# Expert rows as quarter rows, turned by a VectorE block transpose instead of TensorE transposes

## What is computed

```
s = sigmoid(h @ router_w)                    # 384 tokens x 64 experts, 8 chosen per token
for each expert e, on the rows xb of h that chose it:
    y = (silu(xb @ wg[e]) * (xb @ wu[e])) @ wd[e]      # 1024 -> 256 -> 1024
out = swiglu(h, sh_w_gate, sh_w_up, sh_w_down) + sum over a token's experts of weight * y
```

## Time and profile before

| | us |
|---|---|
| runs: median (lowest, highest of 3) | 1751.35 (1750.44, 1751.37) |
| profiled execution: span, first to last instruction | 1745.4 |
| PE busy | 1661.9 (95%) |
| DVE busy | 642.6 (37%) |
| ACT busy | 387.3 (22%) |
| POOL busy | 222.8 (13%) |
| data moved | 530.52 MB |

### The profile page before, as it was taken

The page is one execution under the profiler, slowest core; times in us unless marked ns, Lnnn a source line. Parts: engine busy times, 40 slices in busy tenths (PEclk is TensorE's granted clock), DMA queues, the critical chain, the costliest instruction groups (busy, mean ns, idle before and its releaser), DMA issues.

```text
span 1745.4 us, 22336 instructions
## 1 busy us (share of the span) xinstructions
PE 1661.9 (95%) x8468; PEld 821.2 (47%) x8468; DVE 642.6 (37%) x1697; ACT 387.3 (22%) x842; POOL 222.8 (13%) x217
## 2 busy tenths in 40 slices
PE   4999889989999999999979998998999999999997
PEld 2765344644444444444447553555434444444443
DVE  2479372522222222222256765442322222222222
ACT  2410343221111111111152104431111111111111
POOL 0200010011111111111113000101111111111110
PEclk7999999999999999999989999999999999999999
DMA  9312753399999999999932229017899999999994
GB/s 403 133 54 102 279 210 145 126 403 374 417 403 413 417 388 419 420 420 419 381 128 97 103 97 375 23 60 310 338 418 416 396 420 396 412 419 420 419 420 166
DMA packets 77291, 530.52 MB, mean 304 GB/s; under 512 B 10880, under 2 KB 14080, under 8 KB 21632
## 3 DMA queue, kind: packets, MB, share of 16 engines
q1 hardware_dynamic: 67392, 503.90, 70.7%
q0 software_dynamic: 9792, 25.18, 3.7%
HBM read 533.76 MB, written 5.77 MB: 309 GB/s over the span
## 4 chain that ended last, share of the span: by engine, by line
PE 89%; DVE 4%; DMA 4%; ACT 2%; issue 1%; SPq 0%; POOL 0%; DVEq 0%; ACTq 0%
PE PSB L932 30%; PE PSB L941 15%; PE PSB L924 7%; PE PSB L986 6%; PE PSB L987 5%; PE PSB L974 4%; PE PSB L860 4%; DMA RING<-in_wmod 2%; PE PSB L896 1%; PE PSB L959 1%; PE PSB L919 1%; PE PSB L680 1%; PE PSB L906 1%; PE PSB L897 1%; DMA RING<-in_exp_w_up 1%; PE PSB L948 1%
## 5 line engine op out<-in xcount | busy, mean ns | idle before, releaser
L932 PE MATMUL PSB<-WB,EX 128*32 128x512 f32 (+2 forms) x1408 | 431.9, 598 | 0.6 <-DMA RING<-in_exp_w_up 0.6
L932 PE MATMUL PSB<-RING,EX 128*32 128x512 f32 (+2 forms) x1344 | 417.2, 598 | 1.7 <-DVE EX L1790 1.7
L941 PE MATMUL PSB<-RING,AT 128*32 128x512 f32 (+2 forms) x720 | 227.9, 599 | 4.8 <-ACT GROW L1299 3.7
L1808 DVE TENSOR_TENSOR YL<-PSB,YH 128x512 fp32r<-128x512 f32 x136 | 94.1, 692 | 353.8 <-ACT YH L1380 353.8
L941 PE MATMUL PSB<-WB,AT 128*32 128x512 f32 (+2 forms) x704 | 210.8, 596 | 0.0
L564 POOL TENSOR_SCALAR SCAT<-CST,LSTT 128x384 fp32r<-128x384 f32 x68 | 85.1, 1251 | 833.0 <-PE PSB L987 832.8
L932 PEld LDWEIGHTS PSB<-WB,EX 128*32 128x32 f32 (+2 forms) x1408 | 113.1, 126 | 136.3 <-issue 136.3
L986 PE MATMUL PSB<-YH,SCAT 128*128 128x512 f32 x408 | 171.6, 421 | 2.8 <-DVE YL L1808 2.8
L1790 DVE COPY EX<-PSB 128x512 f32<-128x512 f32 x68 | 47.1, 692 | 317.4 <-PE PSB L974 317.4
L932 PEld LDWEIGHTS PSB<-RING,EX 128*32 128x32 f32 (+2 forms) x1344 | 105.8, 124 | 122.5 <-issue 122.5
L987 PE MATMUL PSB<-YL,SCAT 128*128 128x512 f32 x408 | 161.0, 395 | 0.0
(11 more groups left out here) (286 smaller groups left out, 1856.6 us busy)
## 6 DMA issues: line engine op xcount, KB each, us to landing
RING<-in_exp_w_gate SPq DMA_DIRECT2D x64, 1024.0 KB, 12.4
RING<-in_exp_w_up SPq DMA_DIRECT2D x64, 1024.0 KB, 14.7
RING<-in_exp_w_down SPq DMA_DIRECT2D x64, 1024.0 KB, 13.1
WB<-in_exp_w_gate SPq DMA_DIRECT2D x64, 1024.0 KB, 11.7
WB<-in_exp_w_up SPq DMA_DIRECT2D x64, 1024.0 KB, 14.4
WB<-in_exp_w_down SPq DMA_DIRECT2D x64, 1024.0 KB, 13.3
RING<-in_wmod SPq DMA_DIRECT2D x16, 2048.0 KB, 10.6
KSYS<-in_wmod SPq DMA_DIRECT2D x8, 2048.0 KB, 10.4
```

What stands on the lines that cost most here:

```text
L932: mm = nc.tensor.matmul(PS[6][s0:s0 + w, :].rearrange("p (w f) -> p w f", w=2), e[:, k, s0:s0 + w], rawgu[n % NBUF][:, k], start=(k == 0), ...
L941: mm = nc.tensor.matmul(dst[s0:s0 + w, :], AT[:, j, s0:s0 + w], rawdn[n % NBUF][:, hf, j], start=(j == 0), stop=(j == 1))
L1808: v.tensor_tensor(YLb[s % 2][:, hf * 512:(hf + 1) * 512], PS[6 + hf][:, :], YHb[s % 2][:, hf * 512:(hf + 1) * 512].bitcast(F32), ALU.subtr ...
```

## The change

A row of h is now gathered as four quarter rows of 1 KB. HTOK is written in a permuted order, so that quarter r of a row holds, for each of the eight k-blocks, 32 of its features. The gather uses four indirect DMAs: DMA g fills columns 256g to 256g + 255 of XG, and on partition 32r + j it brings quarter r of the token of slot 32g + j. A transpose of 32x32 blocks on DVE then gives EX2 directly: on partition 32r + i stands feature i of quarter r, and along the free axis the slots 32g + j. IDX becomes four columns, filled by sixteen small DVE operations on 32 partitions each (4 x token + r, from PSUM partitions 32g on to SBUF partitions 32r on). The eight transposes on PE, their copies on ACT and DVE and their semaphores go; PE waits for `d_ex` of the DVE transpose instead. The wait for the second YL half, which stood before the first transposes, stands after gate/up. The same is done in the `more` loop.

```diff
-LSTN, SORTN = 4, 10
+LSTN, SORTN = 19, 10
...
+        h_quarters = h_rows.rearrange("t (r n) -> (t r) n", r=4)
...
-            IDX = sb("IDX", [P, NU], mybir.dt.int32, c=me)
+            IDX = sb("IDX", [P, NU, 4], mybir.dt.int32, c=me)
...
                 pool.wait_ge(d_lst, LSTN * (NU * l + s + 1))
                 if s >= 2:
-                    pool.wait_ge(pe_rows, 2 * (NU * l + s - 1))
-                pool.indirect_dma_start(XG[:, s % 2, :], None, h_rows,
-                                        bass.IndirectOffsetOnAxis(ap=IDX[:, s:s + 1], axis=0),
-                                        bounds_check=TOK - 1, oob_is_err=False).then_inc(rows_in[s % 2], 16)
+                    pool.wait_ge(d_ex, NU * l + s - 1)
+                for g in range(4):
+                    pool.indirect_dma_start(XG[:, s % 2, g * 256:(g + 1) * 256], None, h_quarters,
+                                            bass.IndirectOffsetOnAxis(ap=IDX[:, s, g:g + 1], axis=0),
+                                            bounds_check=4 * TOK - 1, oob_is_err=False).then_inc(rows_in[s % 2], 16)
...
+            def slots(b):
+
+                return lambda k, s0, w: EX2[:, b, k, s0:s0 + w]
...
-            def rows(l, s, h):
-
-                if h == 0:
-                    pe.wait_ge(rows_in[s % 2], 16 * (len(range(s % 2, NU, 2)) * l + s // 2 + 1))
-                else:
-                    pe.wait_ge(e_low, NU * l + s + 1)
-                for c in range(4):
-                    k = 4 * h + c
-                    mm = nc.tensor.transpose(PS[7][:, c * P:(c + 1) * P], XG[:, s % 2, k * P:(k + 1) * P], ident)
-                mm.then_inc(pe_rows, 1)
...
-                pe.wait_ge(e_low, NU * l + s + 1)
-                pe.wait_ge(e_high, NU * l + s + 1)
+                pe.wait_ge(d_ex, NU * l + s + 1)
                 if s > 0:
                     pe.wait_ge(d_yl, 2 * (NU * l + s) - 1)
                 for k in range(KD):
-                    mm = gate_up(job, EX2[:, s % 2], k)
-                    if k == 2 and s + 1 < NU:
-                        if s > 0:
-                            pe.wait_ge(d_yl, 2 * (NU * l + s))
-                        rows(l, s + 1, 0)
-                    if k == 5 and s + 1 < NU:
-                        rows(l, s + 1, 1)
+                    mm = gate_up(job, slots(s % 2), k)
                 mm.then_inc(pe_gu, 1)
-                if s + 1 < NU:
-                    pe.wait_ge(e_high, NU * l + s + 2)
+                if s > 0:
+                    pe.wait_ge(d_yl, 2 * (NU * l + s))
...
-                    own.sig(sc.activation(HTOK[:, t, hf * 512:(hf + 1) * 512], PS[YB[0][t] + hf][:, :], ACT.Copy), a_tk)
+                    own.sig(sc.activation(HTOK[:, t, :].rearrange("p (r k j) -> p k r j", r=4, k=KD)[:, 4 * hf:4 * hf + 4],
+                                          PS[YB[0][t] + hf][:, :].rearrange("p (k r j) -> p k r j", k=4, r=4), ACT.Copy), a_tk)
...
-            def rows(l, s):
-
-                act.wait_ge(pe_rows, 2 * (NU * l + s) + 1)
-                sc.activation(EX2[:, s % 2, 0:4, :].rearrange("p k s -> p (k s)"), PS[7][:, :], ACT.Copy).then_inc(e_low, 1)
...
-                v.tensor_scalar(IDX[:, s:s + 1], PS[7][:, 260:261], NONE, None, ALU.add).then_inc(d_lst, 1)
+                for g in range(4):
+                    for r in range(4):
+                        v.tensor_scalar(IDX[32 * r:32 * r + 32, s, g:g + 1], PS[7][32 * g:32 * g + 32, 260:261],
+                                        4.0, 4.0 * NONE + r, ALU.mult, ALU.add).then_inc(d_lst, 1)
...
-                def high(s):
-
-                    dve.wait_ge(pe_rows, 2 * (NU * l + s + 1))
-                    v.tensor_copy(EX2[:, s % 2, 4:8, :].rearrange("p k s -> p (k s)"), PS[7][:, :]).then_inc(e_high, 1)
-
-                high(0)
+                def turned(s):
+
+                    dve.wait_ge(rows_in[s % 2], 64 * (len(range(s % 2, NU, 2)) * l + s // 2 + 1))
+                    if s >= 2:
+                        dve.wait_ge(pe_gu, NU * l + s - 1)
+                    v.transpose(EX2[:, s % 2].rearrange("p k (g j) -> p g k j", g=4),
+                                XG[:, s % 2, :].rearrange("p (g k j) -> p g k j", g=4, k=KD)).then_inc(d_ex, 1)
+
+                turned(0)
                 for s in range(NU):
                     if s + 3 < NU:
                         onehot(l, s + 3)
                     if s + 1 < NU:
-                        high(s + 1)
+                        turned(s + 1)
```

More of the change, by code:

```diff
@@ L585, in more_pool @@
                                                         ALU.is_equal).then_inc(m.onehot, 1)
-                            after(m.lst, 3 * ((r + gone) * NE + c + 1))
-                            pool.indirect_dma_start(XG[:, 0, :], None, h_rows,
-                                                    bass.IndirectOffsetOnAxis(ap=IDXF[:, 0:1], axis=0)).then_inc(m.rows_in, 16)
+                            after(m.lst, 18 * ((r + gone) * NE + c + 1))
+                            for g in range(4):
+                                pool.indirect_dma_start(XG[:, 0, g * 256:(g + 1) * 256], None, h_quarters,
+                                                        bass.IndirectOffsetOnAxis(ap=IDXF[:, g:g + 1], axis=0)).then_inc(m.rows_in, 16)
                             nc.gpsimd.tensor_scalar(SCAT[:, 0, :], cst("iota"), LF[:, 1:2], None, ALU.is_equal).then_inc(m.scat, 1)
@@ L1105, in mixture_pe @@
                 pe.wait_ge(d_lst, LSTN * (NU * l + 3))
-                rows(l, 0, 0)
-                rows(l, 0, 1)
                 for s in range(NU):
@@ L1124, in mixture_pe @@
                             mm.then_inc(m.lists, 1)
-                            pe.wait_ge(m.lst, 3 * n)
-                            pe.wait_ge(m.rows_in, 16 * n)
-                            for k in range(KD):
-                                mm = nc.tensor.transpose(PS[6 + k // 4][:, (k % 4) * P:(k % 4 + 1) * P], XG[:, 0, k * P:(k + 1) * P], ident)
-                            mm.then_inc(m.rows, 1)
-                            pe.wait_ge(m.e, 2 * n)
+                            pe.wait_ge(m.e, n)
                             pe.wait_ge(m.w_in, 48 * n)
                             for k in range(KD):
-                                mm = gate_up(SHARED, EX2[:, 0], k)
+                                mm = gate_up(SHARED, slots(0), k)
                             mm.then_inc(m.gu, 1)
@@ L1387, in mixture_act @@
                             n = (r + gone) * NE + c + 1
-                            act.wait_ge(m.rows, n)
-                            for h in range(2):
-                                sc.activation(EX2[:, 0, 4 * h:4 * h + 4, :].rearrange("p k s -> p (k s)"), PS[6 + h][:, :],
-                                              ACT.Copy).then_inc(m.e, 1)
                             act.wait_ge(m.gu, n)
@@ L1822, in mixture_dve @@
                             dve.wait_ge(m.lists, n)
-                            v.tensor_copy(IDXF[:, 0:1], PS[7][:, 1:2]).then_inc(m.lst, 1)
+                            for g in range(4):
+                                for q in range(4):
+                                    v.tensor_scalar(IDXF[32 * q:32 * q + 32, g:g + 1], PS[7][32 * g:32 * g + 32, 1:2],
+                                                    4.0, float(q), ALU.mult, ALU.add).then_inc(m.lst, 1)
                             v.tensor_copy(LF[:, 1:2], PS[7][:, 1:2]).then_inc(m.lst, 1)
                             v.tensor_copy(LF[:, 0:1], PS[7][:, 0:1]).then_inc(m.lst, 1)
+                            dve.wait_ge(m.rows_in, 64 * n)
+                            v.transpose(EX2[:, 0].rearrange("p k (g j) -> p g k j", g=4),
+                                        XG[:, 0, :].rearrange("p (g k j) -> p g k j", g=4, k=KD)).then_inc(m.e, 1)
                             dve.wait_ge(m.sig, n)
-                            dve.wait_ge(m.lst, 3 * n)
+                            dve.wait_ge(m.lst, 18 * n)
                             v.scalar_tensor_tensor(out=ACTV, in0=PS[6][:, 0:DE], scalar=LF[:, 0:1], in1=SGM,
```

20 lines of the change are left out of this document (9 added, 11 removed).

## The result

The changed kernel takes 1867.19 us (median of 4 runs, 1860.98 to 1868.11) against 1750.89 for the kernel before beside it: a ratio of 1.066, 95% interval 1.0642 to 1.0678, 116 us slower. The forecast was 1932 in a range of 1835 to 1985. The profiled execution has a span of 1866.0 us against 1745.4.

What follows compares the result with a forecast made beforehand. PE was taken to set the pace, weight loads just keeping up. Transposes −96.4, flip chain +184.1, clock +84.2, layer starts +9.1 gave +181; 1745.4 + 181 + 5.95 = 1932 us, range 1835 to 1985.

Steps and rivals of the forecast that it cites:

- The chain at the flip: Lists to ACTV to flip: sixteen held index instructions, 0.19 us each, add 2.97 us in 62 steps, +184.1 us.
- The transposes: On PE: two groups of four transposes leave each hand-over, 1.46 us a step, 66 times, −96.4 us.
- The clock: PE's clock falls after the new gap in five of six of 62 steps, 1.63 us each, +84.2 us.
- From span to time: The median of the runs stood 5.95 us above the profiled span; this was added at the end.
- Start of a layer: Step 0's later gather and the held shared flip, with one clock fall: 4.5 us a layer, +9.1 us.
- Terms taken as nothing: Block transpose, POOL's four issues, permuted HTOK copies and smaller gather packets: bounded or estimated, but added as zero.
- The block transpose: On DVE after the one-hot: bounded by 0.7 and 2.5 us, up to 5.5 us costing nothing in a step.
- The permuted HTOK copies: Six copies a layer, 0.594 us each before: at most 6 us more, nothing taken.
- Rival 1: At the flip: same chain but the clock stays up, +93.5, 1845 us; chance 0.22.
- Rival 2: At the flip: the sixteen overlap or only a moved input holds; not slower, about 1745 us; chance 0.13.
- Rival 3: At DVE's transpose: gathers land late, everything behind waits, 3.9 us a step, 2174 us; chance 0.09.

Runs made afterwards that it cites:

- l_light: Against the changed kernel: index instructions moved behind the two ACTV operations, only a quarter of w_down loaded except for each layer's first experts; 1663.55 us, ratio 0.9511.
- e_one: Against the changed kernel: the sixteen index instructions of a list become one on 128 partitions, so wrong rows are gathered; 1746.65 us, ratio 0.9984.
- e_busy: Against the changed kernel: ten more scatter-sized matmuls with weights of zero on PE in front of the wait for ACTV; 1834.81 us, ratio 1.0496.
- e_kinds: Against the kernel with one index instruction: fifteen dummies behind it, by step with nothing, the output start or the input start moving; 1788.58 us (one run).

## Why the prediction was right, and where its size was off

- **The chain at the flip: right, in mechanism and nearly in size.** The sixteen take 2.94 us and PE waits 2.50. With the transposes gone and no chain a step is 14.01 (`l_light`); with it 16.78: 2.77 us a step against the forecast's 2.97. The chain itself grew by 2.91 (from the first index instruction to the first ACTV operation it is 3.42 us after and 0.51 before), and 0.08 us was cover that was there before. Its spacing of 0.19 us is 0.185 in the list.
- **The transposes: right.** 1.48 us a step measured, 1.46 forecast. What rows before the change could not show is that the loads take nearly all of it back once the chain is out of the way (1746.65 and 1751.66 us). The forecast allowed 26 us for that, from a DMA share of 0.99 against 1.015 over a stage; that share can't be turned into time so. `e_one`, with no chain and no transposes, has a share of 1.01 over the same stretch and moves the same 409 GB/s as before:

```profile
342.80:869.00 526.20, 485.43 (x2634) 219.61 (x2634) 150.33 (x375) 69.50 (x138) 182.09 (x170) 0.99 1.01 409
```

- **The clock: this step failed by its share.** "I take five in six" of 62 steps at 1.63 us, 84.2 us. Measured: 19 of 62, 31.4 us. The price was right on average (1.65), with some luck, since a typical fall costs 1.3 and three cost 2.7 to 2.9. The share was taken from six single gaps outside the steps, whose surroundings differ; "the new gap is longer than all of them" was no reason for at least the same share, as the table of gaps shows. This is 53 of the 60 us by which the forecast of the span was too high.
- **From span to time.** The 5.95 us were taken as what lies around the span. In the runs on record a time stands 1.8 to 2.0 us above its span (1867.96 against 1866.0); the other 4 are the distance of the profiled execution from the median, which need not recur. So the spans differ by 120.6 us and the medians by 116.3.
- **Start of a layer: right in kind,** 5.4 us for two against 9.1. In both layers PE waits 3.29 us at the shared flip for LSTW, and a granted clock of 0.50 follows, as in this stretch of layer 0:

```profile
358.50:362.00 3.50, 2.85 (x15) 2.76 (x14) 0.52 (x4) 1.04 (x2) 2.89 (x3) 0.50 1.01 400
```

- **Terms taken as nothing.** The block transpose takes 1.24 us, between the bounds of 0.7 and 2.5, and half of the estimate from the Trainium skill, VectorE: DVE Perf Modes, section "The three transpose paths"; no run here has a bf16 one. It waits for the gather twice, 3.1 us in all, and no kernel shows it on the path of a steady step. The permuted HTOK copies take 0.594 us, as before. The gathers' landing fell to 6.2 us from the 8.9 of the earlier trace rows; POOL's issues take 1.0 us each beside other work.
- **Rivals.** Rival 1 (no falls, 1845 us) is what `e_busy` shows, 1834.81. Rival 2 (not slower) is near what `e_one` shows, 1746.65 us, but with one instruction in the place of sixteen; for sixteen that overlap there is only the first kind of `e_kinds`, where fifteen unmoved ones leave a wait of 0.58 us at the flip. Rival 3 did not occur; its 128 packets for a gather are 144 by the queue's line (9792 for 68 gathers).

## What to carry over

A handful of tiny instructions on an idle engine is not free when they stand in the one chain that another engine waits for: ask of each added instruction what is queued behind it, and move what nobody needs yet behind what someone waits for. Instructions on VectorE that hop between start partitions run one after another, so count them at their full spacing (0.16 to 0.185 us here, against 0.07). And before pricing work that leaves a busy engine, take the next bound away in an experiment, or a floor that lies just under the old time will keep the gain (here all but 3 of some 85 us).

## What was not expected of the hardware

- Signals cost spacing: 0.180 us from start to start with a semaphore and 0.162 without, for instructions that are held anyway.
- A quarter of the row size did not mean four times the packets. The page's line for the gather queue (packets, MB, share of 16 engines), after:

```profile
q0 software_dynamic: 13056, 25.22, 4.1%
```

Before it was 9792 packets and 3.7%: 144 packets for a gather of 4 KB rows, 48 for one of 1 KB rows, 192 a step. The queue's time grew by 76.5 - 64.6 = 12 us over the whole span, not fourfold.
- The share of steps with a fall of the clock is no function of the gap alone (the table above), and the falls come back at regular distances; what else sets them stays open.
